# Head norms and rotations in steps between projection blocks and attention units, in a grouped and in a differential attention layer

## What is computed

```python
# layer 0 of the second block: differential attention, 8 heads of 2 x 64
p = jax.nn.softmax(sc, axis=-1)
p = p[:, 0] - lam_full * p[:, 1]
o = jnp.einsum('bhlk,bkhd->blhd', p.astype(vb.dtype), vb)
o = rmsnorm(o, subln) * (1.0 - lambda_init)
# layer 1: grouped attention, 8 query heads, 2 key heads of 128
q = rmsnorm(q.reshape(b, n, GA_KV_HEADS, grp, GA_HEAD_DIM), q_norm)
k = rmsnorm(k.reshape(b, n, GA_KV_HEADS, GA_HEAD_DIM), k_norm)
q, k = apply_rope_2(q, cos, sin), apply_rope_2(k, cos, sin)
```

## Time and profile before

| | us |
|---|---|
| median of 3 runs | 2740.15 (2739.03 to 2740.39) |
| the profiled execution, its own time | 2737.63 |
| its span | 2735.9 |
| TensorE busy | 2561.8 (94%) |
| its weight loads (PEld) | 2427.4 (89%) |
| VectorE (DVE) busy | 1693.4 (62%) |
| ScalarE (ACT) busy | 1239.5 (45%) |
| mean granted TensorE clock | 0.967 |

### The profile page before, as it was taken

How to read it: one execution, slowest core, us unless ns; L and a number is a source line. 1 busy time by engine, 2 the same in 40 slices (tenths; PEclk the granted TensorE clock), 3 DMA queues, 4 the chain that set the end, 5 groups by cost and what they waited for, 6 DMA issues and landing times.

```text
span 2735.9 us, 48496 instructions
## 1 busy us (share of the span) xinstructions
PE 2561.8 (94%) x20634; PEld 2427.4 (89%) x20634; DVE 1693.4 (62%) x2842; ACT 1239.5 (45%) x1668; POOL 1.2 (0%) x6
## 2 busy tenths in 40 slices
PE   6789999999999999999998998999999999887998
PEld 5679998988998899999896898999999999856998
DVE  5565464556666656566767666577655557646655
ACT  4443443444545444454445554445444445434443
POOL 0000000000000000000000000000000000000000
PEclk9889998999999999999998999999999999898999
DMA  6546655533455664544341344554445545353453
GB/s 236 215 172 244 247 189 202 208 109 115 181 192 211 234 242 182 183 154 151 116 158 61 110 176 148 185 185 170 171 169 185 185 174 181 114 197 140 166 181 116
DMA packets 68613, 475.76 MB, mean 174 GB/s; under 512 B 7984, under 2 KB 8496, under 8 KB 14768
## 3 DMA queue, kind: packets, MB, share of 16 engines
q1 hardware_dynamic: 66240, 468.74, 47.8%
q10 hardware_dynamic: 2160, 3.93, 0.4%
...
## 4 chain that ended last, share of the span: by engine, by line
PE 77%; DVE 12%; ACT 5%; DMA 4%; issue 2%; ACTq 0%; DVEq 0%
PE bank L250 66%; ACT whi L209 3%; PE bank L1008 2%; DVE wlo L229 2%; DMA raw<-w_main 2%; DMA raw<-w_down 2%; DVE wlo L216 1%; PE bank L890 1%; PE bank L828 1%; DVE tmpx L613 1%; PE bank L1339 1%; DVE HX L619 1%; DVE ARX L662 1%; PE bank L706 1%; PE bank L744 1%
## 5 line engine op out<-in xcount | busy, mean ns | idle before, releaser
L250 PE MATMUL bank<-HNX_hi,whi 128*128 128x256 f32 x2968 | 865.1, 292 | 57.8 <-DVE wlo L229 17.1
L209 ACT ACTIVATE whi<-raw 128x2048 fp32r<-128x2048 f32 (+1 forms) x378 | 705.6, 1868 | 334.8 <-PE bank L250 182.0
L250 PE MATMUL bank<-HNX_hi,wlo 128*128 128x256 f32 x2968 | 848.2, 287 | 0.0
L250 PE MATMUL bank<-HNX_lo,whi 128*128 128x256 f32 x2968 | 832.9, 286 | 0.0
L216 DVE TENSOR_TENSOR wlo<-raw,whi 128x1024 fp32r<-128x1024 f32 (+1 forms) x378 | 453.4, 1199 | 579.6 <-ACT whi L209 579.3
L250 PEld LDWEIGHTS bank<-HNX_hi,whi 128*128 128x128 f32 x2968 | 580.4, 196 | 82.9 <-issue 43.1
L250 PEld LDWEIGHTS bank<-HNX_hi,wlo 128*128 128x128 f32 x2968 | 581.2, 196 | 0.0
L250 PEld LDWEIGHTS bank<-HNX_lo,whi 128*128 128x128 f32 x2968 | 571.6, 195 | 1.6 <-issue 1.4
L229 DVE TENSOR_TENSOR wlo<-raw,whi 128x1024 fp32r<-128x1024 f32 (+1 forms) x378 | 450.8, 1193 | 0.0
L250 PE MATMUL bank<-HNC_hi,whi 128*128 128x256 f32 x1344 | 390.7, 291 | 7.8 <-DVE tmpc L434 3.5
L250 PE MATMUL bank<-HNC_lo,whi 128*128 128x256 f32 x1344 | 381.9, 284 | 0.0
...
## 6 DMA issues: line engine op xcount, KB each, us to landing
...
```

Source lines behind the costliest of these rows:

```text
L209: NS.activation(WHI[q % HIS][:, 0:size], RAW[m % SLOTS][:, 0:size], ACT.Copy).then_inc(sems["w_hi"], 1)
L250: return NT.matmul(dst, (WHI[ordinal[n] % HIS], WLO[n % SLOTS])[w][:, k * 2 * P + col:k * 2 * P + col + P], x[xp][:, kx, :], start=start, ...
```

## The change

`tile_norm` is no longer used by the x lane in these two layers. A new `head_steps` gives the same norm for one tile or one pair in three steps (squares; totals, root, reciprocal and diagonal; spread and scaling). In the grouped layer they stand between the projection blocks, and the last of them and the turns of the last two pairs between the first units of attention; units wait for the turn of their own pair (`unit_ready`) and not for all. Each head is split two iterations after its second unit. In the differential layer each head is normed during the attention, in iterations 2h+5 to 2h+7, so each has its own root. The attention of the grouped layer uses other banks, and the values of the differential layer are transposed in another order.

```diff
@@ -41,6 +41,20 @@
+class Between:
+    def __init__(self):
+        self.marks, self.later = {}, {}
+
+    def at(self, step, job):
+        self.later.setdefault(step, []).append(job)
+
+    def run(self, step):
+        for job in self.later.pop(step, ()):
+            job()
@@ -806,10 +820,67 @@
                         keep_low(j - 1)
                 return (his, los) if keep else marks[-1]
 
-            def attend(S, units, scale, PB, PT, neg_lam, ready, score_bank, turn_bank, out_bank):
-
-
-                exps, mult, trans, copied, pv, kept = {}, {}, {}, {}, {}, {}
+            def head_steps(S, tiles, gain, factor, square, diag_in, inv_at, totals, spread, kept_by, keep_at=None):
+
+                n = tiles.shape[1]
+                (tb, ta), (sb, sa) = totals, spread
+                totals_, spread_in_ = tb[:, ta:ta + 2 * n], sb[:, sa:sa + n * T]
+                wide = [x.rearrange("p (a q) -> p a q", a=n) for x in (square, diag_in, spread_in_)]
+                inv = SMALL[:, inv_at:inv_at + 2 * n]
+                m = {}
+
+                def squares(*ready):
+                    m["sq"] = up("act_step")
+                    if on(act, *ready, kept_by.get("square")):
+                        NS.activation(wide[0], tiles, ACT.Square).then_inc(m["sq"].sem, 1)
+
+                def scales():
+                    total, root, rec = up("pe_step"), up("act_step"), up("dve_step")
+                    if on(pe, m["sq"], free.get(tb.name)):
+                        for c in range(2 * n):
+                            mm = NT.matmul(totals_[:, c:c + 1], square[:, c * P:(c + 1) * P], ones[:, 0:1], start=True, stop=True)
+                        mm.then_inc(total.sem, 1)
+                    kept_by["square"] = total
+                    if on(act, total):
+                        NS.activation(inv, totals_, ACT.Sqrt, bias=vec("eps6"), scale=1.0 / P).then_inc(root.sem, 1)
+                    free[tb.name] = root
+                    if on(dve, root):
+                        NV.reciprocal(inv, inv).then_inc(rec.sem, 1)
+                        dve.wait_ge(*rec)
+                    if factor is not None:
+                        fac = up("dve_step")
+                        if dve:
+                            NV.tensor_scalar(inv, inv, factor, None, MUL).then_inc(fac.sem, 1)
+                            dve.wait_ge(*fac)
+                    m["diag"] = up("dve_step")
+                    if on(dve, kept_by.get("diag")):
+                        NV.tensor_tensor(diag_in.rearrange("p (c q) -> p c q", c=2 * n), ident.unsqueeze(1).to_broadcast([P, 2 * n, P]),
+                                         inv.unsqueeze(2).to_broadcast([P, 2 * n, P]), MUL).then_inc(m["diag"].sem, 1)
+
+                def normed():
+                    sp_, sc = up("pe_step"), up("dve_step")
+                    if on(pe, m["diag"], free.get(sb.name)):
+                        NT.matmul(spread_in_, ones, diag_in, start=True, stop=True).then_inc(sp_.sem, 1)
+                    kept_by["diag"] = sp_
+                    if on(dve, sp_):
+                        NV.scalar_tensor_tensor(tiles, tiles, gain, wide[2], MUL, MUL).then_inc(sc.sem, 1)
+                    free[sb.name] = sc
+                    m["done"] = sc
+                    if keep_at is not None:
+                        hi, lo = up(f"{S.tag}_hn_hi"), up(f"{S.tag}_hn_lo")
+                        if on(act, sc):
+                            NS.activation(S.HN[0][:, keep_at:keep_at + n, :], tiles, ACT.Copy).then_inc(hi.sem, 1)
+                        if on(dve, hi):
+                            NV.tensor_tensor(S.HN[1][:, keep_at:keep_at + n, :], tiles, S.HN[0][:, keep_at:keep_at + n, :].bitcast(fp32), SUB)\
+                                .then_inc(lo.sem, 1)
+                        m["done"] = lo
+                return squares, scales, normed, m
+
+            def attend(S, units, scale, PB, PT, neg_lam, ready, score_bank, turn_bank, out_bank, between, unit_ready=None):
+
+
+                exps, mult, trans, copied, pv = {}, {}, {}, {}, {}
+                kept = between.marks
                 last, base = len(units), S.col + 12
 
                 def small_(at, u, n=2):
@@ -817,11 +888,12 @@
                 NEGM, MAXM, SUM, CO = 0, 6, 12, 18
                 for it in range(last + 3):
                     u, x1, w, r = it, it - 1, it - 2, it - 3
+                    between.run(it)
                     if u < last:
                         yield ("L", 1.2, 3.0)
                         q, ks, vs, parts, dst = units[u]
                         np_, sc = len(parts), up("pe_step")
-                        if on(pe, *ready, *(free.get(score_bank(u, a)[0].name) for a in range(np_))):
+                        if on(pe, *ready, *(unit_ready(u) if unit_ready else ()), *(free.get(score_bank(u, a)[0].name) for a in range(np_))):
                             for a, pr in enumerate(parts):
                                 bank, c0 = score_bank(u, a)
                                 for c, k in enumerate(ks):
@@ -1584,17 +1656,27 @@
                 vt = None
                 for m, t in todo:
                     roped = turn(Z[:, t:t + 2, :], *ROT, side[t // 2 % 2], t // 2, m)
-                vt = by_token([Z[:, 16 + h, c * P:(c + 1) * P] for c in range(2) for h in range(8)], VTX, side, z_v)
+                vt = by_token([Z[:, 16 + h, c * P:(c + 1) * P] for h in range(8) for c in range(2)], VTX, side, z_v)
                 want("kv0")
                 hold_bank()
                 both = (slice(0, 64), slice(64, P))
-                units = [(Z[:, h, qt * P:(qt + 1) * P], [Z[:, 8 + h, :], KC[:, h, :]], [VTX[:, 8 * c + h, :] for c in range(2)] + [VC[:, 8 * c + h, :] for c in range(2)],
+                units = [(Z[:, h, qt * P:(qt + 1) * P], [Z[:, 8 + h, :], KC[:, h, :]], [VTX[:, 2 * h + c, :] for c in range(2)] + [VC[:, 8 * c + h, :] for c in range(2)],
                           both, YX[:, h, qt * P:(qt + 1) * P]) for h in range(8) for qt in range(2)]
+                between, shared, steps = Between(), {}, []
+                for h in range(8):
+                    steps.append(head_steps(X, YX[:, h:h + 1, :], vec("subln"), 1.0 - LAMBDA_INIT, SQX[0], SQX[1], 96 + 2 * h,
+                                            (BANK[5], P), (BANK[5], T), shared, h))
+                    between.at(2 * h + 5, lambda h=h: steps[h][0](between.marks[2 * h + 1]))
+                    between.at(2 * h + 6, steps[h][1])
+                    between.at(2 * h + 7, steps[h][2])
                 o = yield from attend(X, units, 0.125, PB, PT, LAM, [roped, vt, *kv_ready["kv0"]],
-                                      lambda u, a: (BANK[2 * (u % 2) + a], 0), BANK[4], BANK[5])
+                                      lambda u, a: (BANK[2 * (u % 2) + a], 0), BANK[4], BANK[5], between)
+                passed.add("x_da")
+                while between.later:
+                    between.run(min(between.later))
+                    yield ("L", 1.5)
                 paused.discard("a")
-                passed.add("x_da")
-                x = yield from tile_norm(X, [YX[:, h:h + 2, :] for h in range(0, 8, 2)], lambda h: vec("subln"), 1.0 - LAMBDA_INIT, [o], vec("eps6"), BANK[4], BANK[2:4], True)
+                x = None, [m["done"] for *_, m in steps]
                 free["x", "gain"] = need(0, 5)
                 y = yield from linear(X, "da_out", OUT, None, ready=x[1], gain=post(X, 0, 1))
                 mods = need(0, 6, 7)
@@ -1617,25 +1699,51 @@
                 if on(act, *y):
                     act.dma_start(CS, A["tab_ga"]).then_inc(in_tab.sem, 16)
                 x = yield from norm(X, True, pre(X, 1, 1), y, mods)
-                z = yield from linear(X, "ga_in", [(0, 0), (1, 2), (2, 4), (3, 6), (4, 8), (5, 10)], Z, first=x)
+                z = yield from linear(X, "ga_in", [(0, 0), (1, 2)], Z, first=x)
                 vt = by_token([Z[:, 2 + g, c * P:(c + 1) * P] for c in range(2) for g in range(2)], VTX, side[:1], z[1])
-                normed = [0, 4, 6, 8, 10]
-                nqk = yield from tile_norm(X, [Z[:, t:t + 2, :] for t in normed], lambda j: vec("k_norm" if j < 2 else "q_norm"), None, [z[-1], vt],
-                                           vec("eps6"), BANK[4], BANK[2:4])
+                ROT = (vec("rot_ax"), CS[:, 0, :], CS[:, 1, :])
+                shared, roped = {}, {}
+                tiles = [0, 4, 6, 8, 10]
+                steps = [head_steps(X, Z[:, t:t + 2, :], vec("q_norm" if t else "k_norm"), None, TMPX[0][:, :], SQ2[:, :], 96 + 4 * i,
+                                    (BANK[3], 0), (BANK[2], 0), shared) for i, t in enumerate(tiles)]
                 if dve:
                     dve.wait_ge(*in_tab)
-                ROT = (vec("rot_ax"), CS[:, 0, :], CS[:, 1, :])
-                for j, t in enumerate(normed):
-                    roped = turn(Z[:, t:t + 2, :], *ROT, side[j % 3], j, nqk)
+
+                def rotate(i):
```

(31 more changed lines are left out.)

## The result

The changed kernel takes 2752.66 us (median of 7 runs, 2747.70 to 2759.69), the kernel before 2739.20 (median of 7, 2736.66 to 2740.39). The ratio is 1.0049 with a 95% interval of 1.0040 to 1.0059: 13.5 us slower, where 2723 was forecast, outside the range of 2713 to 2737. The profiled execution took 2752.66, its span is 2750.9 against 2735.9, so the two traces differ by 15.0 us at the end.

A forecast was written before the change was run, and what follows sets the result against it. TensorE, busy 94% of the span, was taken as the bound, with gains only where it idles or runs slow. 10.1 + 5.5 + 2.5 + 1.6 + 2.0 - 4.5 = 17.2 us less gave 2723 as median, range 2713 to 2737.

The forecast's parts named there:

- Differential attention, cost 4.5, bounds 0 and 25: Differential attention: head steps entering its pipeline cost 4.5 us, 3.0 at the start and 1.5 near 1540, none between.
- The old head norm cost TensorE nothing: Behind differential attention: 192 context products lay among the old norm's totals and spreads, so replacing it gains nothing.
- Front, gain 10.1: Grouped layer, last projection to first turned unit: 16.9 us of idle or slow clock shrink to 6.8; bounds 4 and 14.
- (b): Grouped layer's front: the context's 96 products come in one piece and their bare chain of waits costs 3.2 us.
- Behind, 5.5: Behind grouped attention: splitting head by head gains 2.9 us idle and 2.6 us clock; bounds 2.9 and 5.6.
- The norms: Gains around norms: 2.5 us ahead of the grouped layer, 1.6 after its output projection, 2.0 after the differential one.
- Front gain lost: Rival: low clock lasts into grouped attention, front gains 4, differential cost 9, 2733 us; chance 0.18 shared with another rival.
- ScalarE the bound: Rival in differential attention: seven heads' roots and table loads delay exp, 24 us plus 4 for VectorE, 2746 us; chance 0.10.
- Longer loads: Rival: table loads hold ScalarE about twice as long as their rows show, 13 us in differential attention, 2736; chance 0.04.
- Steps are no cover: Rival at grouped projection blocks: VectorE's waits delay weight splits, eating 6 to 10 us, near 2733; chance 0.18 shared.

The follow-up runs named there:

- the run that won 15.7 us: Differential layer's change alone, its steps moved behind each unit's scores and softmax work, ahead of its transposes, against the kernel before: 2737.64 us, ratio 0.9992.
- the last experiment: Whole change with steps behind the unit's softmax work and room for more context products behind differential attention, against the kernel before: 2717.07 us, ratio 0.9922.
- the change with room: Whole change with room for more context products behind differential attention, no other edit, against the kernel before: 2735.93 us, ratio 0.9986.
- the kernel before with room: Kernel before with only room added for more context products behind differential attention, against the kernel before: 2739.83 us, ratio 1.0000.

## Why the prediction was wrong

**"Differential attention, cost 4.5, bounds 0 and 25": this step failed.** Measured are 26 us for the layer where it ends, the 2.0 gained in the norm behind it included; some 10 come back later, and the layer's change alone costs the kernel 15.1. The forecast had 3.0 us for the start, nothing from 1480 on and 1.5 near the end. The attention grew by 29.0, and against the kernel before, by the transposes of the seventh and fourteenth units, 12.4 of them fall to the start, 7.9 to the steady part and 8.7 to the end. I had VectorE's added work right (1.6 us a head) and in a rival even named that it "stands in line for the root", but priced that wait once, as 1.4 us, and as if it ended there. It is 2.0 us a head on average (16.0 in eight), another 12.7 stand ahead of the scalings, which I had not counted at all, and what I missed is that it closes a loop over TensorE and ScalarE back to itself, so that in the first units nothing absorbs it. Nor did I look at which bank the totals use. From 1480 on I said that TensorE bounds the stretch and drew from it that steps cost nothing. The cover that I relied on did hold there, no transposes wait for VectorE; but TensorE, the bound engine, was the one on which the steps stand, behind a product whose copy they need: 0.70 us a unit, and 0.3 to 0.4 for the step itself. The attention's 29.0 us, by TensorE's timeline: 7.9 more of waits for the bank (8.4 for 0.5), 2.1 more for VectorE's L914, 1.0 for the root, 7.7 for totals and spreads, and the rest, some 10, the lower clock and the ends of value products that nothing overlaps. "The old head norm cost TensorE nothing" was nearly right (leaving it out gains 8) and should have warned me: there was little to gain here.

**"Front, gain 10.1": this step failed too**, by the term (b). I took the context's 96 products as ready when their turn came and costed their bare chain at 3.2. The norm ahead of them was itself behind four steps of the latent sequence on VectorE: 7.20 us idle, 12.2 in all between the norm and the first turned unit where it had been 8.4, at the same mean granted clock (0.87 in both). The stretch became 2.3 us longer, a gain of -2.3 instead of 10.1. The bound of 14 "if no spell comes" is what it reaches once the context is ahead: 85.4 to 73.9 is 11.5, with ten more x products inside the second (2.5 us in the kernel before, 2334.24 to 2336.78). I ought to have asked for the stretch's late guest: the work that `want` forces in there.

**"Behind, 5.5": right** within a us for what it counted. Idle 4.03 to 1.73, first products 8.38 to 5.99: 4.7. What I costed at nothing, the attention itself, was not nothing: 63.9 to 69.8 us. On TensorE it holds two turns and a spread that stood ahead of it before (2.6 us) and one modulation block more (1.0), but also 2.8 us more idle; the splits alone account for 2 of the 6.

**The norms: right.** Ahead of the grouped layer the idle pieces sum to 5.3 us for 7.5, so 2.2 (2.5 forecast). After the differential output projection it is 3.56 for 5.54, 2.0 as forecast. From the grouped output projection's start to the first product behind its norm 43.9 us pass for 48.3; less the clock gain of 2.4 counted above, 2.0 (1.6 forecast).

**The rivals.** *Front gain lost* came true in size and beyond, by a wait and not by the clock. (The wait of 1.9 us that it read in today's chain is 1.46 us of idle on TensorE.) *ScalarE the bound* had the right sign and half of the size (6 us slower for 13.5). Its price, the seven roots' loads, was the wrong one: without any load for the root the kernel gains 4.2 of the 14 us. Of its chain, exp behind the root, then VectorE's scaling, then the transposes, the part on ScalarE was undone together with VectorE's in the run that won 15.7 us, so that part stays open. 53 table loads for 39 are there as foreseen; the units 8.35 us apart are not (9.47 to 9.49), and from the context's last product to the first turned unit 20.0 us pass for 24.6, where 16 to 19 were forecast. *Longer loads* is out: at 1467.83 a load, directly behind a copy, at 1469.13 the root, 1.30 us as in the earlier trace rows; the 2.66 that the Trainium skill gives (ScalarE: Activation LUTs, "What ACT_TABLE_LOAD costs") is not seen here either. *Steps are no cover* is out: no wait for a weight split stands among the grouped projections; VectorE's order did hold something back, but it was the context's norm. With the two failed steps mended, in the last experiment, the kernel takes 2717, 22 us under the kernel before where the sum said 17; the grouped attention, 5.2 us shorter there than in the change with room, is in no term of the sum, so the agreement of the rest is good to a few us and no better.

What stays open: the steps behind differential attention are 6 us under the kernel before with room, and 7.5 us lie between the two kernels with the grouped change that are built on them. The ones with room have 550 context products behind the attention and not 454, and their norm is in one piece; which of the two it is was not tried.
